# Gated scan on one core: the query side of every level moved from VectorE to GpSimd

## The reference, cut to what matters

```python
def step(S, inp):                      # one chunk of 64 tokens, scanned over chunks
    b = jnp.cumsum(gc, axis=2)
    diff = b[:, :, :, None, :] - b[:, :, None, :, :]
    decay = jnp.exp(jnp.where(mask, diff, -jnp.inf))
    scores = jnp.einsum("bhtk,bhsk,bhtsk->bhts", qc, kc, decay)
    o = (jnp.einsum("bhts,bhsv->bhtv", scores, vc)
         + jnp.einsum("bhtk,bhkv->bhtv", qc * jnp.exp(b), S))
    ...
o_f, s_f = _gla_scan(qh, heads(kf), heads(gf), vh, s0_f)
o_b, s_b = _gla_scan(flip(qh), flip(heads(kb)), flip(heads(gb)), flip(vh), s0_b)
return o_f + flip(o_b), s_f, s_b
```

## Time and profile before

| | |
|---|---|
| median of 3 runs | 2869.01 us (2867.65 to 2870.35) |
| the profiled execution's own time | 2868.01 us |
| its span | 2866.2 us |
| PE (TensorE matmul) busy | 2667.0 us, 93% |
| PEld (weight load) busy | 2321.4 us, 81% |
| DVE (VectorE) busy | 1177.1 us, 41% |
| ACT (ScalarE) busy | 1068.2 us, 37% |
| POOL (GpSimd) busy | 688.5 us, 24% |

### The profile page before, as it was taken

One profiled execution on the slowest core, in us unless ns is written; L12 is line 12 of the kernel. 1 busy time (PEld: TensorE's weight loads), 2 busy tenths in 40 slices (PEclk: granted clock), 3 DMA queues, 4 the chain that ended last, 5 costly groups with the idle time before them and its releaser, 6 DMA issues. The chain is left out here.

```text
span 2866.2 us, 42736 instructions
## 1 busy us (share of the span) xinstructions
PE 2667.0 (93%) x16745; PEld 2321.4 (81%) x16745; DVE 1177.1 (41%) x1766; ACT 1068.2 (37%) x1474; POOL 688.5 (24%) x276
## 2 busy tenths in 40 slices
PE   6999898999889999989999989889999589996999
PEld 3888686988868888768888688779989489995999
DVE  3222224237642222242222356743354636634644
ACT  2322233535333222243222346445454344443433
POOL 0222121220012222212222213024434024440343
PEclk8999999999999999989999999999999789997999
DMA  5343353330023333434333424035555025551454
GB/s 228 133 168 138 125 145 114 122 132 1 30 103 139 133 132 132 147 105 145 132 132 132 168 85 162 6 118 176 178 201 190 30 96 180 181 177 44 149 188 148
DMA packets 57279, 375.37 MB, mean 131 GB/s; under 512 B 6159, under 2 KB 10919, under 8 KB 12872
## 3 DMA queue, kind: packets, MB, share of 16 engines
q1 hardware_dynamic: 56092, 371.58, 36.3%
q10 hardware_dynamic: 1068, 2.11, 0.6%
HBM read 370.51 MB, written 3.16 MB: 130 GB/s over the span
## 5 line engine op out<-in xcount | busy, mean ns | idle before, releaser
L1317 POOL TENSOR_TENSOR WL<-RAW,WH 128x1024 fp32r<-128x1024 f32 x272 | 688.3, 2530 | 2164.9 <-ACT WH L972 2164.9
L972 ACT ACTIVATE WH<-RAW 128x1024 fp32r<-128x1024 f32 x544 | 545.6, 1050 | 1075.0 <-PE PSA L512 1067.2
L1340 DVE TENSOR_TENSOR WL<-RAW,WH 128x1024 fp32r<-128x1024 f32 x272 | 346.7, 1275 | 1279.2 <-ACT WH L972 1279.1
L510 PE MATMUL PSA<-HH,WH 128*128 128x256 f32 (+1 forms) x2400 | 817.9, 341 | 25.3 <-DVE HL L1423 23.5
L511 PE MATMUL PSA<-HL,WH 128*128 128x256 f32 (+1 forms) x2400 | 807.9, 337 | 0.0
L512 PE MATMUL PSA<-HH,WL 128*128 128x256 f32 (+1 forms) x2400 | 806.5, 336 | 0.0
L510 PEld LDWEIGHTS PSA<-HH,WH 128*128 128x128 f32 x2400 | 459.8, 192 | 89.9 <-issue 43.2
L510 PE MATMUL PSA<-GH,WH 128*128 128x256 f32 (+1 forms) x1536 | 506.2, 330 | 7.0 <-DVE GL L1358 7.0
L511 PE MATMUL PSA<-GL,WH 128*128 128x256 f32 (+1 forms) x1536 | 498.8, 325 | 0.0
L512 PE MATMUL PSA<-GH,WL 128*128 128x256 f32 (+1 forms) x1536 | 498.5, 325 | 0.0
L512 PEld LDWEIGHTS PSA<-HH,WL 128*128 128x128 f32 x2400 | 459.6, 192 | 46.9
(11 more groups left out here) (254 smaller groups left out, 2207.0 us busy)
## 6 DMA issues: line engine op xcount, KB each, us to landing
RAW<-in_weights SPq DMA_DIRECT2D x272, 1024.0 KB, 4.8
ADA<-in_w_ada SPq DMA_DIRECT2D x65, 1024.0 KB, 4.8
Zada<-in_w_ada SPq DMA_DIRECT2D x7, 1024.0 KB, 13.4
scratch_bias<-BREL ACTq DMA_DIRECT2D x1, 2048.0 KB
SUMS<-in_c_sums SPq DMA_DIRECT2D x1, 1664.0 KB, 8.4
TB<-scratch_bias SPq DMA_DIRECT2D x1, 1536.0 KB, 11.5
X<-in_x SPq DMA_DIRECT2D x1, 1024.0 KB, 8.2
X<-in_ctx SPq DMA_DIRECT2D x1, 1024.0 KB, 12.2
```

What stands on the lines that cost most here:

```text
L510: pe.matmul(out, a_hi, b_hi, start=start, stop=False)
L972: act.activation(WH[:, j, 4 * h:4 * h + 4, :], RAW[:, j, 4 * h:4 * h + 4, :], ACT.Copy)\
L1317: pool.tensor_tensor(WL[:, j, 4:8, :], RAW[:, j, 4:8, :], WH[:, j, 4:8, :].bitcast(F32), ALU.subtract)\
L1340: dve.tensor_tensor(WL[:, j, 0:4, :], RAW[:, j, 0:4, :], WH[:, j, 0:4, :].bitcast(F32), ALU.subtract)\
```

## The change

GpSimd makes the query side: `right` and `carried` move from VectorE's list to a `mixer` in GpSimd's, word for word but for the engine. `lr_ready` becomes two semaphores, `left_ready` (VectorE, after the second product of `left`; for the diagonal an empty instruction) and `right_ready` (GpSimd). TensorE's scores and ScalarE's exponentials wait for both. VectorE keeps `left`, `pick` and `KS`, in their order. GpSimd's loop over the slots is cut where a mixer stands; the slots up to the second of the phase behind the mixer are split before it, the rest after it. Products, operands and tiles are the same.

```diff
@@ TensorE, scores(g)
                     for v in range(2):
-                        n.take(lr_ready)
+                        n.take(left_ready)
+                        n.take(right_ready)
@@ ScalarE, level_exps(g)
                     if g >= 2:
-                        act.wait_ge(lr_ready, lrs + 2 * (g - 1))
+                        act.wait_ge(left_ready, lefts + 2 * (g - 1))
+                        act.wait_ge(right_ready, rights + 2 * (g - 1))
@@ GpSimd
-            repeat(pool, SLOTS // 2, two_slots, first=1)
+
+            n = Tally(pool)
+
+            def mixer(ph):
+                tbs = 4 if ph["layer"] == 0 else 2
+                for p in range(2):
+                    pool.wait_ge(bank_read[p], ph["unit"] + BANK_CREDIT)
+                n.skip(exp_ready, len(CHAIN))
+                scored = n.at(score_ready)
+
+                def right(g, v):
+                    tb, level = g // 4, 2 * (g % 4) + v
+                    for d in range(2):
+                        half = 1 - d
+                        q = Q[:, :, P * tb:P * tb + P].rearrange("p h (a two m) -> p h a two m", two=2, m=1 << level)
+                        r = RQ[:, g % 2, v].rearrange("p h (a two m) -> p h a two m", two=2, m=1 << level)
+                        e = E[:, g % 2, d, v].rearrange("p h (a two m) -> p h a two m", two=2, m=1 << level)
+                        ins = pool.tensor_tensor(r[:, :, :, half, :], e[:, :, :, half, :], q[:, :, :, half, :], ALU.mult)
+                    ins.then_inc(right_ready, 1)
+
+                def carried(g):
+                    tb = g // 4
+                    if tb:
+                        n.take(o_ready)
+                    for d in range(2):
+                        ins = pool.tensor_tensor(QHAT[d], E[:, g % 2, d, 1], Q[:, :, P * tb:P * tb + P], ALU.mult)
+                    ins.then_inc(right_ready, 1)
+
+                for g in range(4 * tbs):
+                    n.take(exp_ready, 4)
+                    if g >= 2:
+                        pool.wait_ge(score_ready, scored + 2 * (g - 1))
+                    for v in range(2):
+                        if 2 * (g % 4) + v < LEVELS:
+                            right(g, v)
+                        else:
+                            carried(g)
+                n.skip(score_ready, 8 * tbs)
+                n.skip(o_ready)
+
+            done = 2
+            for ph in PLAN:
+                if ph["kind"] == "mixer":
+                    split = PLAN[PLAN.index(ph) + 2]["slot"] + 2
+                    repeat(pool, split // 2, two_slots, first=done // 2)
+                    mixer(ph)
+                    done = split
+            repeat(pool, SLOTS // 2, two_slots, first=done // 2)
@@ VectorE, mixer: right and carried go, and
                     for v in range(2):
-                        last = g % 4 == 3 and v == 1
-                        if not last:
+                        if 2 * (g % 4) + v < LEVELS:
                             left(g, v)
+                        else:
+                            dve.engine_nop().then_inc(left_ready, 1)
                         if g:
                             pick(g - 1, v)
-                        (carried(g) if last else right(g, v))
```

More of the change, by code:

```diff
@@ L343, in build @@
         ke_ready, u_ready, state_ready = sem("ke_ready"), sem("u_ready"), sem("state_ready")
-        lr_ready, score_ready, picked = sem("lr_ready"), sem("score_ready"), sem("picked")
+        left_ready, right_ready = sem("left_ready"), sem("right_ready")
+        score_ready, picked = sem("score_ready"), sem("picked")
         kt_ready, kf_ready = sem("kt_ready"), sem("kf_ready")
@@ L1185, in mixer @@
                 split_hi(16 * ((slot + 1) // 2 + 1), 1)
-                lrs = n.at(lr_ready)
+                lefts, rights = n.at(left_ready), n.at(right_ready)
                 def k_copy(tb):
@@ L1215, in mixer @@
                         copy_out(g // 4 - 1)
-                n.skip(lr_ready, 8 * tbs)
+                n.skip(left_ready, 8 * tbs)
+                n.skip(right_ready, 8 * tbs)
                 copy_out(tbs - 1)
@@ L1732, in flat @@
                     return x.rearrange("p h t -> p (h t)")
-                lrs, scored, picks = n.at(lr_ready), n.at(score_ready), n.at(picked)
+                scored, picks = n.at(score_ready), n.at(picked)
                 def left(g, v):
@@ L1739, in left @@
                         half = d
[L1740 to L1760, removed]
+                        ins = dve.tensor_tensor(halves(flat(LK[:, g % 2, v]), level)[:, :, half, :],
+                                                halves(flat(E[:, g % 2, d, v]), level)[:, :, half, :],
+                                                halves(KK[:, d, tb, :], level)[:, :, half, :], ALU.mult)
+                    ins.then_inc(left_ready, 1)
                 def pick(g, v):
@@ L1789, in mixer @@
                     pick(groups - 1, v)
-                n.skip(lr_ready, 2 * groups)
                 n.skip(score_ready, 2 * groups)
                 n.skip(picked, 2 * groups)
-                n.skip(o_ready)
                 n.take(o_read, tbs)
```

## The result

| | before | after |
|---|---|---|
| median of 10 runs | 2870.07 us (2867.42 to 2876.45) | 2878.45 us (2875.49 to 2880.49) |
| profiled execution, span | 2868.01, 2866.2 us | 2880.44, 2878.6 us |

The ratio is 1.0026 (95% interval 1.0016 to 1.0036): slower by 0.26%, some 7.5 us. The forecast was 2871.5 (+2.5), and what came is the first rival's size.

A forecast was written before the change was run, and what follows sets the result against it. TensorE's pace was taken as the bound, with 7.3 us of waits for VectorE the most to win. Layer 0 +1.15 and layer 1 +1.35 gave +2.5 us: 2870.5 profiled, median 2871.5, range 2866 to 2884.

The forecast's parts named there:

- first rival: Short GpSimd products cost 0.72 us or more, slowing heads and groups before outputs: over 5.7 us, +11 at 0.80; chance 0.25.
- ceiling: TensorE's waits for VectorE in both layers' scans, 7.3 us, are the most the change can win.
- Turns: VectorE's key products and GpSimd's products wait for each other's whole instruction; key products rise from 418 to 700 ns or more.
- third rival: The engines take no turns and work at the same time: -3.6 us, 2865.4; chance 0.08.
- price of a product: A GpSimd query product was taken at 0.65 us, a carried one at 1.2, a key product behind GpSimd about 0.28.
- head: First groups of a layer, without copies to hide anything: second half later, partly regained from the fourth group, +0.85 us a layer.
- upper bound of 0.80: Highest price for a GpSimd query product, 0.57 plus 0.23 us of start, if none of the start hides.
- ordinary group: Key product first, then query, alternating: halves ready at 1.92 and 3.8 us, where before 2.0 and 4.0.
- middle blocks: Products, copies and KS fit in TensorE's 20.7 us block; two such blocks in layer 0 give -0.2 us.
- last group: End of each layer's scan, no cover: diagonal scores at 759.9 in place of 759.38, +0.5 us a layer.
- forecast of no change: Time within 0.2%, 5.7 us, of the kernel before; chance 0.57.
- second rival: Unfair turns: GpSimd keeps its turn through four products, a group takes 5.1 us in place of 4.0, 2881; chance 0.13.

The follow-up runs named there:

- e7: Changed kernel with VectorE's key products made only for the first two groups of each layer and left out after; 2871.97 us, one run.
- e2: Changed kernel with five idle matmuls into an unread bank before each score half of a layer's last group; 2875.85 us, 1.0022 to before.
- e3: Kernel before, with VectorE making the two carried products of each layer's last group twice; 2879.07 us, 1.0032 to before.
- e8: Kernel before with last-group carried products made twice and five idle matmuls before each score half of that group; 2872.82 us, 1.0008 to before.
- e5: Kernel before with TensorE's first down projection matmuls moved into its waits at each layer's scan end; 2861.53 us, 0.9968 to before.
- e6: Changed kernel with TensorE's first down projection matmuls moved into its waits at each layer's scan end; 2864.33 us, 0.9986 to before.
- e10: The division of work of e9, with down projection matmuls moved into the waits of the last group; 2862.92 us, 0.9972 to before.
- e4: Kernel before with only the 12 carried products moved to GpSimd, the levels' query products staying on VectorE; 2873.29 us, 1.0015 to before.
- e9: Changed kernel with query products of each layer's first three and last groups, and last carried products, back on VectorE; 2874.65 us, 1.0015 to before.
- e1: Changed kernel with query and carried products of each layer's last group back on VectorE; 2872.96 us, 1.0014 to before.

## Why the prediction came out as it did

**What bounds the kernel, and the ceiling on the gain.** Of the 7.3 us that VectorE's list could win none came, so no run tests that ceiling.

**Turns.** Right, and shown in the trace: key products 800 ns for 418, copies unchanged. In e7, where little is left to take turns with, each block behind the first is shorter than in the kernel before, and the layer 0 scan ends at 75.00 against 76.29. It leaves out the key products too, so it does not show what the third rival would have been worth.

**The price of a product.** Nearly right on average, too low where it counts. In turns the head's eight products and their key products took 7.62 us, 0.95 a pair, where the sum had 0.65 + 0.28 = 0.93. But the four pairs of levels 0 and 1 took 4.04 us of it (685.36 to 689.40), 1.01 a pair, and those of levels 2 and 3 0.90. So the second half of the first group started 0.37 us later than the 3.86 forecast, and nothing came back behind it. Alone a product takes 0.82 at levels 0 and 1, a little above the upper bound of 0.80, and 0.70 at the others, between the bounds. The short runs, of which the prediction said that nothing was known, cost 0.12 us a product. A carried product took 1.25, for 1.2. The Trainium skill's figure in "GPSIMD Engine Reference" (performance versus the Vector engine), an estimate of 0.55 us, is under what e7 shows.

```profile
685.36 2.08 POOL L1347 TENSOR_TENSOR RQ<-E,Zfm 128x256 f32<-128x256 f32 x2 [5.55 <-ACT E L1202]
```

**The ordinary group: the step that failed.** The prediction let the key product go first (key, query, key, query), so that the copy for the first half ran from 1.27 and the second half was ready at 3.8. In the first group of each later block GpSimd goes first (703.67 against 703.69, 724.34 against 724.35, 745.50 against 745.51), the second key product waits for two query products, and each copy stands behind it on VectorE's list: 4.7 us, above the 3.6 to 4.5 that TensorE gives. The second half's copy is what TensorE waits for in its list of waits ("DVE PS"), not the query products. So the "middle blocks" cost 0.59, 0.45 and 0.47 us in layer 0 and 0.61 in layer 1, 2.1 us in all, where the sum had -0.2. That a block has room for its turns was right (VectorE is idle for 2.37 us before the group shown above), the order within a group was not. These are the groups of levels 0 and 1 again, so the price has a part in it: with pairs of 1.01 us and the key product first the second half would be ready near 4.1 us (an estimate by the prediction's own walk), so of the 0.9 us between 3.8 and 4.7 the order makes the larger part. No run changed the order alone. The head is another step: it cost 1.40 and 1.36 us for the forecast 0.85. There VectorE goes first, as forecast; the price of the first group makes it, and the 0.35 us that were to come back from the fourth group on did not.

**The last group.** Right: first half 2.08 us after the products began (forecast 1.92), diagonal scores 4.43 (forecast 4.4, from 755.49 to 759.9), 0.54 and 0.52 us later than before (forecast 0.5).

**What was missing: the clock.** The sum had TensorE's work behind the scan move with it at an unchanged rate. In the changed kernel it runs at the lower level for a while: two matmuls of the output start every 0.43 us (768.08, 768.50), which is the 1.2 GHz level, where the same two took 0.22 at 2.4 GHz, an output earlier:

```profile
756.90 0.39 PE L791 MATMUL PSA<-PS,Ztm 128*128 128x128 f32 x2
...
757.12 0.39 PE L793 MATMUL PSA<-ST 128*128 128x128 f32 x2
```

In the profiled executions the two tails lost 1.58 + 1.59 us so, and layer 0's down projection 1.6 us behind that. Over many runs e2 puts it at 2.6 us by the medians, the difference that idle matmuls make, and at 1.1 by the ratios. Waits of 5.9 us and a clock of 2.6 us make 8.5; the medians differ by 8.4, the ratio says 7.5. The clock's share of the median is thus the least certain part of this account; that a fall costs time is clear in e3 and e8, 9.5 and 2.7 us with the same lateness and intervals that do not overlap.

What decides about the clock is only partly shown. No fall was seen in the tails of the ten scans whose end was filled (e2, e5, e6, e8, e10, two layers each). Of the fourteen with waits open, nine fell (both in the changed kernel, e3, e4 and e9, one in e7) and five did not (before, e1, one in e7), and e1 and e9 have the same waits at the end (1.5 and 0.7 us) with opposite outcome. The count depends on where the tail is said to end. In the 14 us behind it the granted clock is 0.88 in layer 1 of the kernel before and of e7, and in layer 0 of e8, which is filled. And one and the same kernel differs from execution to execution: the 23 of the kernel before that ran beside e5 to e8 go from 2867.29 us with a mean clock of 0.962 to 2877.50 with 0.957, so a single profiled execution does not tell what its kernel does as a rule. The Trainium skill ("TensorE: Matmul & The Clock Gate", on the HAM clock gate) has the clock follow TensorE's own recent activity, on a count that runs free of the kernel. The runs agree with the first half of that; the second would fit e1 and e9 and the spread of the kernel before, but no run singles it out.

**Range and chances.** 2878.45 lies inside 2866 to 2884; slower had 0.38 and the forecast of no change 0.57, and the measured 0.26% is just beyond the 0.2% that parted them. That the time lies in the range is partly luck: a clock that the sum did not have is in it. The first rival came near in size (0.72 us or more a product: over 5.7 us), and in part by its mechanism: short runs are slow at levels 0 and 1, 0.82 us, but not at the others, and the order came on top. Of what came beyond the forecast, 2.3 us are the middle blocks, 1.1 the heads (2.76 for 1.7) and 2.6 the clock. The second rival, that GpSimd keeps its turn through all four products, is wrong: two of GpSimd's, never four, end ahead of the second key product at 746.55. Its consequence, VectorE's list stretched to near 5 us a group, came at 4.7.

## What to carry to other kernels

Before a product of two SBUF tensors goes from VectorE to GpSimd, look in the trace for a row where both run at once. If they take turns, the work moved comes back as waiting on the engine that it left, in whole instructions, and what is queued behind the second turn (here the copy that frees a bank) is late. List both orders of who starts first and take the worse. Then look at what TensorE does at the end of a stage where it waits for others: work of a later stage that is ready already can stand in those waits, which was worth 8.6 us here, more than any division of VectorE's work.

## What the runs showed of the hardware that was not expected

Ends of two scans that came 2.9 us later in all cost 9.5 us (e3), and 2.7 us when idle matmuls stood in TensorE's waits (e8): the rest went with TensorE's clock, 0.54 and 0.67 of full behind the waits. Equal waits are not followed by an equal clock (e1 and e9, one execution each). GpSimd's products of 128x256 in runs of 1 and 2 elements take 0.82 us and in runs of 4 to 64 0.70 (e7), while VectorE takes 397 to 426 ns at every level.
